# The state-space scan of a two-block network: its small matmuls in column strips of 32, with the outputs laid out by channel

## The reference, cut to what matters

```python
def s5_mixer(h, ...):
    proj = h @ w_in
    u, z = proj[..., :SSM_WIDTH], proj[..., SSM_WIDTH:]
    ug = uf.reshape(bsz, seq, SSM_GROUPS, SSM_GROUP)      # 64 groups of 16 channels
    ...                                                    # in_re, in_im: B u, scaled
    _, _, s_re, s_im = lax.associative_scan(_complex_linear_combine, (a_re_t, a_im_t, in_re, in_im), axis=1)
    y = einsum('blgp,gcp->blgc', s_re, c_re) - einsum('blgp,gcp->blgc', s_im, c_im)
    y = y.reshape(bsz, seq, SSM_WIDTH) + d_skip * uf
    y = jax.nn.gelu(y)
    y = y * jax.nn.sigmoid(y @ w_glu + b_glu)
    y = y.astype(h.dtype) * jax.nn.silu(z)
    return y @ w_out
```

## Time and profile before

| | us |
|---|---|
| median of 3 runs | 1353.59 (1352.93 to 1358.55) |
| the profiled execution | 1355.93 |
| its span, first to last instruction | 1354.1 |
| TensorE busy | 1333.1 (98%) |
| VectorE busy | 860.0 (64%) |
| ScalarE busy | 715.9 (53%) |

### The profile page before, as it was taken

One profiled execution on the slowest core, in us unless ns is written; L12 is line 12 of the kernel. 1 busy time (PEld: TensorE's weight loads), 2 busy tenths in 40 slices (PEclk: granted clock), 3 DMA queues, 4 the chain that ended last, 5 costly groups with the idle time before them and its releaser, 6 DMA issues.

```text
span 1354.1 us, 23214 instructions
## 1 busy us (share of the span) xinstructions
PE 1333.1 (98%) x10110; PEld 1230.2 (91%) x10110; DVE 860.0 (64%) x1003; ACT 715.9 (53%) x954; POOL 54.8 (4%) x70
## 2 busy tenths in 40 slices
PE   6998999999999999999999999999999999999998
PEld 6998889889999989998999998999989999899997
DVE  6999775756555577767645547555466858655553
ACT  5998566655444463375544445444465355544443
POOL 1002000000000003100000000000000500000000
PEclk9999999999999999999999999999999999999999
DMA  9116555455555564455655565556565546555552
GB/s 271 62 32 212 159 199 187 136 179 172 187 190 198 203 205 169 152 190 184 201 187 187 187 208 182 187 190 199 199 205 193 175 133 203 193 187 187 187 187 93
DMA packets 180297, 242.28 MB, mean 179 GB/s; under 512 B 7547, under 2 KB 144005, under 8 KB 180197
## 3 DMA queue, kind: packets, MB, share of 16 engines
q1 hardware_dynamic: 178260, 234.92, 52.6%
q0 software_dynamic: 1648, 5.67, 1.5%
q10 hardware_dynamic: 288, 0.22, 0.0%
HBM read 239.74 MB, written 1.05 MB: 178 GB/s over the span
## 4 chain that ended last, share of the span: by engine, by line
PE 89%; DVE 9%; issue 1%; DMA 1%; ACT 0%; DVEq 0%; ACTq 0%; POOLq 0%
PE P L415 87%; PE P L450 1%; DVE QQ L1761 1%; DMA G<-in_norm_g 1%; DVE YG L1740 0%; DVE WB L1751 0%; DVE QQ L1765 0%; DVE WL L1445 0%; DVE TMPC L1712 0%; DVE TMPC L1709 0%; DVE QQ L1752 0%; DVE X L1725 0%; DVE TMPD L1678 0%; DVE TMPD L1710 0%; DVE DB L1969 0%
## 5 line engine op out<-in xcount | busy, mean ns | idle before, releaser
L1445 DVE TENSOR_TENSOR WL<-RAW,WH 128x2048 fp32r<-128x2048 f32 x214 | 485.7, 2277 | 305.9 <-ACT WH L1013 304.7
L415 PE MATMUL P<-RH,WH 128*128 128x256 f32 x1856 | 516.8, 278 | 4.3 <-DVE RL L1448 3.0
L415 PE MATMUL P<-RL,WH 128*128 128x256 f32 x1856 | 513.8, 277 | 0.0
L415 PE MATMUL P<-RH,WL 128*128 128x256 f32 x1856 | 513.7, 277 | 0.0
L1013 ACT ACTIVATE WH<-RAW 128x2048 fp32r<-128x2048 f32 x214 | 406.4, 1903 | 194.1 <-DMA RAW<-in_ffn_w_down 82.5
L415 PEld LDWEIGHTS P<-RH,WH 128*128 128x128 f32 x1856 | 348.9, 188 | 6.8 <-DVE RL L1448 2.3
L415 PEld LDWEIGHTS P<-RL,WH 128*128 128x128 f32 x1856 | 348.6, 188 | 1.5
L415 PEld LDWEIGHTS P<-RH,WL 128*128 128x128 f32 x1856 | 348.9, 188 | 0.0
L415 PE MATMUL P<-WH,HLO 128*128 128x512 f32 x352 | 138.7, 394 | 0.0
L415 PE MATMUL P<-WL,HHI 128*128 128x512 f32 x352 | 138.1, 392 | 0.0
L415 PE MATMUL P<-WH,HHI 128*128 128x512 f32 x352 | 137.1, 389 | 0.0
(11 more groups left out here) (306 smaller groups left out, 1376.7 us busy)
## 6 DMA issues: line engine op xcount, KB each, us to landing
RAW<-in_ffn_w_gate SPq DMA_DIRECT2D x88, 512.0 KB, 4.3
RAW<-in_ffn_w_up SPq DMA_DIRECT2D x88, 512.0 KB, 5.7
RAW<-in_ffn_w_down SPq DMA_DIRECT2D x44, 1024.0 KB, 5.0
RAW<-in_w_in SPq DMA_DIRECT2D x36, 1024.0 KB, 5.2
RAW<-in_attn_w_in SPq DMA_DIRECT2D x16, 1024.0 KB, 5.3
RAW<-in_ssm_w_in SPq DMA_DIRECT2D x8, 1024.0 KB, 9.6
RAW<-in_w_out SPq DMA_DIRECT2D x8, 1024.0 KB, 5.1
RAW<-in_ssm_w_glu SPq DMA_DIRECT2D x4, 1024.0 KB, 6.9
```

The source lines that it names most:

```text
L415: return nc.tensor.matmul(*a, **k)
L1445: V.tensor_tensor(WL[:, s, 0:width], RAW[:, s, 0:width], WH[:, s, 0:width].bitcast(f32), SUB).then_inc(sem["lo_split"], 1)
```

## The change

`states_in` and `states_out` use matmuls with 32 columns of weights in place of 128, four times as many. In `states_out` they are also placed differently: strip `q` of 32 PSUM partitions now holds the 32 channels of block `4 m + q`, and step `i` goes along the row, at column `256 m + 64 i`. With that the bank already has 128 channels on its partitions, and one activation of 128 x 512 per batch makes `YG`. `lift` goes, with its semaphore, and with it the second activation. In the last batch the split of unit 9 on ScalarE stands ahead of `y_out(3)`; before it stood between the two parts of it.

```diff
+            def strips(o, lh, rh):
+                for q in range(0, 128, 32):
+                    last = mm(o[q:q + 32], lh[:, q:q + 32], rh, start=True, stop=True, skip_group_check=True)
+                return last
...
-                        last = mm(PP[2 + b % 2][:, ri * 512 + jj * NCH:ri * 512 + jj * NCH + NCH], BT[:, ri, j, :], X4[:, j, :],
-                                  start=True, stop=True)
+                        last = strips(PP[2 + b % 2][:, ri * 512 + jj * NCH:ri * 512 + jj * NCH + NCH], BT[:, ri, j, :], X4[:, j, :])
...
-                for jj in range(JB):
-                    j = JB * b + jj
-                    mm(own(jj), TZ[:, j, :], X4[:, j, :], start=jj == 0, stop=False, skip_group_check=True)
+                for m in range(2):
+                    for i in range(CL):
+                        for q in range(4):
+                            j = JB * b + 4 * m + q
+                            mm(own(m, q, i), TZ[:, j, 32 * i:32 * i + 32], X4[:, j, :],
+                               start=m == 0 and i == 0, stop=False, skip_group_check=True)
...
+                for m in range(2):
+                    for i in range(CL):
+                        for ri in range(2):
+                            for q in range(4):
+                                jj = 4 * m + q
+                                last = mm(own(m, q, i), CP[:, ri, JB * b + jj, i, :], u[:, ri, jj, :], start=False,
+                                          stop=m == 1 and i == CL - 1 and ri == 1, skip_group_check=True)
...
-                for q in range(4):
-                    for i in range(LIFT[b]):
-                        dst = YG[32 * q:32 * q + 32, 2 * b:2 * b + 2, :].rearrange("p m (c i) -> p i m c", i=CL)[:, i]
-                        src = P[Y_BANK[b]][32 * i:32 * i + 32].rearrange("p (m q c) -> p q m c", m=2, q=4)[:, q]
...
+                dst = YG[:, 2 * b:2 * b + 2, :].rearrange("p m (c i) -> p m i c", i=CL)
+                src = P[Y_BANK[b]].rearrange("p (m i c) -> p m i c", m=2, i=CL)
+                fn(dst, src, ACT.Gelu_apprx_tanh).then_inc(sem["y_raw"], 1)
...
             for b in range(NB):
-                y_out(b, split_hi if b == NB - 1 else None)
+                if b == NB - 1:
+                    split_hi()
+                y_out(b)
                 y_high(b)
...
-            lift(NB - 2)
             split_lo()
             for b in range(NB):
-                if b == NB - 1:
-                    lift(b)
                 eng.wait_ge(sem["r_hi"], dve.next("r_hi"))
```

More of the change, by code:

```diff
@@ L28 @@
 G_BANK = [0, 2, 3, 1]
-LIFT = [4, 4, 2, 2]
 HEAD = 16
@@ L264, in build @@
             q_made angle_in sines_there f_there small_there b_there cx_there b_turned c_turned bt_there c_there k_there lags_there lags_copied lags_full compact_there ub_cleared tz_there tz_cleared
-            frac_there table_there in_there in_read unrotated y_raw powers_there x4_there_a x4_there_b x4_there_v gain_d_there params_there c_powers b_summed c_summed c_spread y_lifted dec_cleared dec_there scanned x_again
+            frac_there table_there in_there in_read unrotated y_raw powers_there x4_there_a x4_there_b x4_there_v gain_d_there params_there c_powers b_summed c_summed c_spread dec_cleared dec_there scanned x_again
             glu_sig y_gated y_hi y_lo r_hi r_lo qk_squared qk_rms qk_scaled qk_roped qk_turned qk_there gains_in rope_there
@@ L584, in states_out, with own @@
                 u = (UBA, UBB)[b // 2][:, b % 2]
-                def own(jj):
-                    return P[Y_BANK[b]][:, jj * NCH:jj * NCH + NCH]
-                for jj in range(JB):
-                    j = JB * b + jj
-                    mm(own(jj), TZ[:, j, :], X4[:, j, :], start=jj == 0, stop=False, skip_group_check=True)
+                def own(m, q, i):
+                    c = m * T + i * NCH
+                    return P[Y_BANK[b]][32 * q:32 * q + 32, c:c + NCH]
+                for m in range(2):
[4 more added lines that the diff above has]
+                               start=m == 0 and i == 0, stop=False, skip_group_check=True)
                 if b == 0:
@@ L1158, in toeplitz, with y_out @@
                            ACT.Copy).then_inc(sem["tz_there"] if lag == CL - 1 else act.raised(), 1)
-            def y_out(b, between=None):
+            def y_out(b):
                 eng.wait_ge(sem["y_summed"], b + 1)
-                for q in range(4):
-                    for i in range(LIFT[b]):
-                        dst = YG[32 * q:32 * q + 32, 2 * b:2 * b + 2, :].rearrange("p m (c i) -> p i m c", i=CL)[:, i]
-                        src = P[Y_BANK[b]][32 * i:32 * i + 32].rearrange("p (m q c) -> p q m c", m=2, q=4)[:, q]
[L1167 to L1175, removed]
+                dst = YG[:, 2 * b:2 * b + 2, :].rearrange("p m (c i) -> p m i c", i=CL)
+                src = P[Y_BANK[b]].rearrange("p (m i c) -> p m i c", m=2, i=CL)
+                fn(dst, src, ACT.Gelu_apprx_tanh).then_inc(sem["y_raw"], 1)
             def y_high(b):
@@ L1731, in lags_back @@
                 V.tensor_copy(KTS[:, 0:4, :], P[2].rearrange("p (m l) -> p m l", m=4)).then_inc(sem["lags_full"], 1)
[L1733 to L1740, removed]
             def rows_of(i, b):
```

## The result

| | before | after |
|---|---|---|
| median, us | 1354.40 (1352.93 to 1358.55, 20 runs) | 1351.43 (1348.82 to 1355.22, 20 runs) |
| profiled execution / its span, us | 1355.93 / 1354.1 | 1351.66 / 1349.3 |
| TensorE busy, us (records) | 1333.1 (10110) | 1317.6 (11070) |
| first matmul of unit 9, us | 130.61 | 126.83 |

The ratio of after to before is 0.9979, with a 95% interval of 0.9973 to 0.9986: 2.8 us faster (3.0 by the medians) where 6.0 was forecast. In the two profiled executions unit 9 begins 3.8 us earlier, not 6.0, and behind it the time is the same within 1 us: span less that start is 1223.5 us before and 1222.5 after.

A forecast was written before the change was run, and what follows sets the result against it. TensorE was taken to bound everything from unit 9's start at 130.61 us; shorter sums, one GELU and no lifts bring it to 124.6, 6.0 us less: 1347.6 us against 1353.59, own range 1345 to 1350, 8 in 10 1344.8 to 1351.8.

The forecast's parts named there:

- What bounds the kernel: Whole kernel: TensorE, 98% busy, bounds nearly everything after unit 9 starts at 130.61 us; the change gains what it moves that start.
- Step 1: TensorE, states_in and states_out: a strip costs 15.2 ns, so 19.5 us against 35.6, 16 us less.
- Step 2: TensorE, states_out: most of the 16 us becomes waits; last CP part starts at 114.8, sums at 117.0 instead of 120.32.
- The sign that was named: TensorE, last CP part of states_out(3): the forecast is wrong if it takes over 3 us.
- Step 3: ScalarE behind the sums: split first (1.98 us), then one GELU of 1.1 us; RH starts at 120.2 instead of 126.17.
- Step 4: VectorE: lifts go, RH to unit 9 stays 4.44 us; unit 9 starts at 124.6, 6.0 us less.
- Rival 1: TensorE strips cost 27.5 ns as in lags; unit 9 at 128.4, 2.2 us less, 1351.4 us; chance 0.14.
- Rival 2: TensorE's clock falls in the new waits before states_out(2)'s and (3)'s second halves; 4 us less, 1349.6; chance 0.13.
- Rival 3: TensorE's instruction packets come too slowly for strips; slower if stalls exceed 1.9 us per packet, 1378 at 4.3; chance 0.04.
- The range: Whole kernel time: forecast's own range 1345 to 1350 us; 8 in 10 range 1344.8 to 1351.8, including rivals.

The follow-up runs named there:

- full4_swap: The change with states_in at full width in all batches and ScalarE's y_out(3) and y_high(3) before unit 9's split; 1351.65 us, 0.9964 of the kernel before.
- in_full3: The change with states_in back at full width in the first three batches, the fourth in strips; 1359.41 us, 0.9999 of the kernel before.
- change_again: The change itself run once more, unaltered, as reference on the same chip; 1353.78 us, 0.9973 of the kernel before.
- in_strips_only: The kernel before with only states_in in strips, states_out, lifts and GELUs as before; 1359.13 us, 1.0006 of the kernel before.
- in_full4: The change with states_in back at full width in all four batches, states_out still in strips; 1351.38 us, 0.9949 of the kernel before.
- quiet_loads: The change with unit 12's load and the second load of x held back until the last states_out; 1352.54 us, 0.9961 of the kernel before.
- spaced_23: The change with unit 9's load released by states_out(1), those of units 10 and 11 together by states_out(2); 1351.37 us, 0.9964 of the kernel before.
- swap_spaced_23: spaced_23 with ScalarE's y_out(3) and y_high(3) ahead of the split of unit 9; 1352.22 us, 0.9968 of the kernel before.
- spaced_again: Repeat of the change with the loads of units 9, 10 and 11 released one by one, not together; 1351.17 us, 0.9961 of the kernel before.

## Why the prediction was right or wrong

- **What bounds the kernel:** right for this pair, where the time behind the start of unit 9 stayed within 1 us. It is no exact rule: over the 14 profiles that remainder is 1221.0 to 1225.4 us in twelve and 1228.2 and 1230.0 in `full4_swap` and `in_full3`, which stays open.
- **Step 1:** right in its price, 14.5 ns against 15.2, and in the sum: TensorE is 15.5 us less busy (1333.1 - 1317.6) against 16 forecast.
- **Step 2 failed.** "It would reach the second half of `states_out(2)` and `(3)` some 3.5 us before VectorE has the states", and the last part "takes 128 x 15.2 ns + 0.2 = 2.1 us, not 3.74". TensorE reached them 0.6 us before, since four and five breaks of 1.5 to 2.4 us stood ahead, and the last part took 4.2 us (115.24 to 119.46), with 1.93 without an instruction in it. The sums stood at 119.46, 2.46 us behind the forecast's 117.0: 1.93 of the break, 0.4 of a later start (VectorE was late by as much at 50 us, ahead of the core), 0.1 of the strips. Steps 3 and 4 gave 0.2 back. That is the 2.2 us missing at unit 9 (126.83 for 124.6). The sign that was named, over 3 us for the last `CP`, is the one that came. The medians show another 1 us less gain than the profiled pair; the second profile of the change, with unit 9 at 127.82, is 1 us later by a last part that begins 0.5 us later, a break of 2.10 and 22 records at the lower clock.
- **Step 3:** right. `YG` of 128 x 512 with the strided output took 1.05 to 1.16 us in the timelines (forecast 1.1, bounds 0.6 and 1.7).
- **Step 4:** right in its parts, from `RH` to unit 9 4.3 us against 4.44, and right as a whole once the break was gone (124.53).
- **Rival 1** (27.5 ns a strip) came true in its rate and not in its mechanism: 3.45 us for 128 pairs is 27 ns. That its time, 1351.4, is the measured one is luck: the sums came at 119.46, not 120.8, and unit 9 at 126.83, not 128.4. I had taken the 27.5 ns of `lags` as the price of 128 moving columns. In `lags` a page lasts 3.5 us, just the time in which the next one comes, so by this estimate that row could not have shown a break.
- **Rival 2** (clock) is real, and comes mostly from the breaks, not from the waits that I had looked at (in `in_strips_only` it followed a wait of 2.58 us): it was seen in `change_again`, `in_full3`, `in_full4`, `quiet_loads`, `spaced_23`, `swap_spaced_23` and `in_strips_only`, during a break or a wait or within 1.5 us of its end. The changed kernel's first profile had full clock and missed the forecast all the same, so it is the smaller part.
- **Rival 3** named the mechanism that decided, priced it as a mishap of 4.3 us a packet, and gave it 0.04. The real price was 1.5 to 2.4 us a packet, near its break-even of 1.9, but most of the packets lie ahead of slack. What I missed is that it need not beat the whole gain: one break inside the last part costs its own length. "Fetching ahead during the waits is free" holds for one page only, and the last part of 128 records crosses the end of a page.
- **The range:** 1351.43 lies outside the forecast's own 1345 to 1350 and just inside the 8 in 10, 1344.8 to 1351.8, at the end that was there for the rivals. Its upper term was also added wrongly: a GELU of 1.7 us gives 1347.6 + 0.6 = 1348.2, not 1348.6.

The Trainium skill ("Runtime: NRT & Kernel Launch", Instruction fetch mechanics) says that an engine fetches the next 16 KiB block while it executes the current one and that crossing a boundary is mostly hidden. The trace agrees on the block (16 KB for 128 pairs) and on one block ahead, not on the cost: with pairs at 15 ns each crossing showed as 1.5 to 2.4 us, and up to 5.09 under loads. The 25 ns between starts that the Trainium skill gives ("TensorE: Matmul & The Clock Gate", Back-to-back issue gap) is not borne out by the 14.5 ns here either, though the average with the breaks, 27 ns, is near it.

## What to carry to other kernels

Making matmuls smaller has a second price beside their duration: the instructions. Here 128 pairs of load and matmul cost at least 3.45 us to supply, so anything under 27 ns a pair runs ahead only as far as what is already loaded, the page in use and at most the next; count the pairs between two waits on the path, and see where pages end. Keep large loads out of the few microseconds before such a part, one by one rather than together: a wait on a semaphore in the loads' queue, no work removed, was worth about as much here as the change itself (2.4 to 3.4 us and 2.7 to 3.0 by the medians).

## What was unexpected of the hardware

- The next packet starts only 1.1 us after the page before it is begun, though the engine had waited: 91.22 to 92.3, 94.67 to 95.8. It is usable 2.3 to 2.6 us after its start, of which the transfer is 0.9 to 1.2.
- Beside large loads the packet came later: that of the last part started some 2.5 us after the page before it was begun in the changed kernel and 4.3 us in `spaced_23` (DMA share 1.01 to 1.07), against 0.7 in `spaced_again` and `quiet_loads`; the pages' beginnings are estimates by counting records.
- Breaks can feed on themselves: a break moves TensorE later, the next packet with it, into the next load (argued from the traces, not tested by itself). And in or just behind breaks of 2.1 to 5.1 us the granted clock fell to 0.50, in some executions and not in others, and the 16 `XN` matmuls took up to 5.68 us instead of 3.72.
- Strips of 32 columns on 64 moving ones start every 14.5 ns, four at a time, against 111 ns for a full-width record: 58 ns for the four.
